# Two state-space chunks, or two input steps, in each interruption of TensorE's main stream

## The chip, the cores and the metric

The kernel runs on one core of one Trainium2 chip. The time is that of one launch on the device, in microseconds (us); lower is better. The core's engines are TensorE (PE), VectorE (DVE), ScalarE (ACT), GpSimd (POOL) and SyncE (SP). They run apart from each other and meet at semaphores. A chip run gives a median of several launches; a profile is one more launch, recorded instruction by instruction.

## The reference, cut to what matters

The program is a decoder trunk of two layers over 256 positions of width 2048. Layer 0 mixes positions with two kinds of attention, layer 1 with a state-space bank (S5) and a short convolution. After each mixer come a cross-attention into 256 memory tokens and a squared-ReLU MLP of width 8192. What the change touches is the state-space part:

```python
a_bar = jnp.exp(lam * step)
b_bar = ((a_bar - 1.0) / lam)[..., None] * lax.complex(b_re, b_im)
bu = jnp.einsum('blgc,gpc->blgp', uf, b_bar)
...
states = associative_scan(combine, (a_seq, bu))     # x[t] = a_bar * x[t-1] + bu[t]
y = jnp.einsum('blgp,gcp->blgc', states, c_mat).real + d_skip * uf
```

There are 64 groups of 16 channels and 64 complex states each. All else is matrix products of 256 rows with large weights.

## The kernel before

**Main stream.** Each weight matrix is read in slabs of 1 MB. A slab serves two *halves*; eight halves make a *unit*. For every half ACT copies the raw weights to a rounded part (`whi`, line 1282), DVE subtracts to get the remainder (`wlo`, line 1854), and TensorE multiplies with both (lines 635 to 637, or 1108 and 1111 in units that put the weights in the stationary place). The buffers hold four halves. So ACT may split half t only when TensorE is done with half t-4 (semaphore `half_used`), and TensorE may begin half t only when `wlo` of t is there (`lo_ready`). SP issues the slabs, each when `wlo` of the half that last used its place has been made.

**Side work.** A number t counts halves from a stage's start; after the split or the products of half t each engine calls what is due at t. Each engine's list is fixed in the program text, so an instruction that waits holds back all that stands behind it on its engine, the next split included.

**Tables.** The state-space tables depend only on parameters and are built beside the last chunks but one of layer 0's MLP (four chunks of four units, t = 0 to 127), in 16 *chunks* k of two group pairs each. For a chunk DVE makes the real parts in four pieces from t = 30 + 6k (`re_tables`, lines 1954 to 1973, semaphore `s5_re`) and POOL the imaginary parts (lines 2548 and 2779, `s5_im`). Both use the buffers k % 2. TensorE then visits (`s5_chunk`, after half 33 + 6k): 4 small fp32 matmuls into one bank of `at`, in 8 passes. At t = 37 + 6k ACT waits until the store of the chunk before has landed (`k_out`), copies half of the bank (line 1387), stores `et_d` and `ca_d` (lines 1389, 1392), waits until DVE has added the other half (lines 1932, 1935, `k_sum`), and stores `k_d` (two DMAs, line 1395). The buffers of chunk k are free for chunk k + 2 when TensorE has visited k and its stores have landed; SP loads the factors of chunk k (line 479) at t = 28 + 6k, once chunk k - 2 has used its own.

**Steps.** In layer 1's input projection (t from its first unit) TensorE makes the states' inputs in 8 *steps* (`s5_x`, after halves 27 to 34): 16 small matmuls, 32 passes, into one bank of `at`. ACT copies a step's bank three halves later in its own list (line 1353). SP loads the tables of step k (`et_d`, 0.5 MB, line 550) into a ring of three buffers, three steps ahead at most: step k waits for TensorE's step k - 3. The output steps (`s5_y`) already run two per visit, after halves 53, 55, and so on.

**Hidden sums.** In the MLP's second and third unit, DVE adds the two parts of the hidden products (line 2236), and ACT makes relu and two squares (lines 1639 to 1642), at fixed halves in the same lists (halves 2 and 4 of the unit).

Of the kernel before, what the change touches and what calls it, by code (L numbers as in the profile page):

```python
# [44 lines left out]
G, GC, ST = 64, 16, 64  # L45
Q = G // 2
T8 = 8
J = L // T8
# [57 lines left out]
def trunk(nc, x, mem, norm_mix, norm_xattn, norm_mlp, norm_mem, norm_final, ab_w_in, ab_b_forget,  # L106
# [4 lines left out]
    with ctx:  # L111
# [52 lines left out]
        etab = view(1024, 1024, "p (b q r w) -> p b q r w", b=2, q=2, r=2)  # L164
# [13 lines left out]
        cz = [view(at_, 576, "p (q r w) -> p q r w", q=2, r=2) for at_ in (7616, 10240)]  # L178
# [36 lines left out]
        S = view(2112, 2048, "p (r j q) -> p r j q", r=2, q=Q)  # L215
# [31 lines left out]
        at = ctx.enter_context(nc.psum_tensor("at", [P, 2, NB], F32))  # L247
# [4 lines left out]
        et_d = nc.dram_tensor("et_d", [P, Q, 2, GW], F32, kind="Internal").ap()  # L252
        ca_d = nc.dram_tensor("ca_d", [2, P, Q, GW], F32, kind="Internal").ap()
# [44 lines left out]
        s5_re, s5_im = sem("s5_re"), sem("s5_im")  # L298
# [33 lines left out]
        TAB_CHUNKS = (3, 4, 5, 6)  # L332
        FACTOR_T, STORE_T = (0, 2, 4), 16
        DVE_T = [32 + 6 * k - 2 for k in range(16)]
        CHUNK_T = [32 + 6 * k + 1 for k in range(16)]
        ROWS_T, SIN_T = 8, 29
        X8_T, SCAN_T, Y_T = 25, 39, 53
        SWAP_T = (49, 51, 52)
# [251 lines left out]
        def _(pe):  # L590
            p = Place()
# [186 lines left out]
            def s5_chunk(k):  # L778

                b = k % 2  # L780
                pe.wait_ge(s5_re, k + 1)
                pe.wait_ge(s5_im, k + 1)
                bank = open_at()
                for r in range(2):
                    for q in range(2):
                        ln = 2 * GC * (2 * r + q)
                        last = mm(bank[ln:ln + 2 * GC, 0:GW], eb[:, b, q, r, :], cz[b][:, q, r, 0:GW])
                close_at(last)
# [6 lines left out]
            def s5_tables(t):  # L795
                if t in FACTOR_T:
                    s5_factors(FACTOR_T.index(t))
                if t in CHUNK_T:
                    assert p.n["at"] == at_before_tab + CHUNK_T.index(t)
                    s5_chunk(CHUNK_T.index(t))  # L800

            for u in range(4):
                def after(i, u=u):
# [399 lines left out]
                close_at(last)  # L1203

            def s5_steps(t):
                if 0 <= t - X8_T - 2 < 8:
                    s5_x(t - X8_T - 2)
                if 0 <= t - Y_T < 16 and (t - Y_T) % 2 == 0:
                    s5_y(t - Y_T)
                    s5_y(t - Y_T + 1)  # L1210
# [49 lines left out]
        def _(act):  # L1260
# [87 lines left out]
            def at_copy(copies):  # L1348

                n = p.n["at"]  # L1350
                act.wait_ge(at_full, n + 1)
                for dst, src in copies(at[:, n % 2, :]):
                    last = act.activation(dst, src, ACT.Copy)
                last.then_inc(at_free[n % 2], 1)
                p.bump("at")
# [20 lines left out]
            def s5_tables(t):  # L1376

                if t - 4 in FACTOR_T:
                    at_copy(lambda bank: [(fput[FACTOR_T.index(t - 4)], bank)])
                if t - 4 not in CHUNK_T:  # L1380
                    return
                k = CHUNK_T.index(t - 4)
                b = k % 2
                n = p.n["at"]
                act.wait_ge(*((k_out, 32 * k) if k else (ksb_zero, 1)))
                act.wait_ge(at_full, n + 1)
                act.activation(ksb[:, 112:240], at[2 * 2 * GC:P, n % 2, 0:GW], ACT.Copy).then_inc(k_part, 1)
                p.bump("at")
                act.dma_start(et_d[:, 2 * k:2 * k + 2].rearrange("p q r w -> p (q r w)"),
                              etab[:, b].rearrange("p q r w -> p (q r w)")).then_inc(et_out[b], 16)  # L1390
                for r in range(2):
                    act.dma_start(ca_d[r, :, 2 * k:2 * k + 2], cz[b][:, :, r, GC:]).then_inc(ca_out[b], 16)
                act.wait_ge(k_sum, k + 1)
                for q in range(2):
                    act.dma_start(k_d.rearrange("c (s k q) w -> k q s c w", s=2, q=2)[k, q],
                                  ksb[2 * GC * q:2 * GC * (q + 1), :]).then_inc(k_out, 16)
# [308 lines left out]
            def s5_slots(t):  # L1705
                if t in SWAP_T:
                    swap_states(SWAP_T.index(t))
                k = t - 5 - X8_T
                if 0 <= k < 8:

                    at_copy(lambda bank: [
                        (S[:, r, :, 4 * k:4 * k + 4].rearrange("p j q -> p q j"),
                         bank[:, 0:8 * J].rearrange("p (q r j) -> p r q j", q=4, r=2)[:, r])
                        for r in range(2)])
                k = t - 3 - Y_T
                if 0 <= k < 16:
                    b = k % YB
                    if k >= YB:
                        act.wait_ge(y_out[b], 16 * (k // YB))
                    at_copy(lambda bank: [  # L1720
                        (Yc[:, b, :, q * GC:(q + 1) * GC], bank[2 * J * q:2 * J * (q + 1), 0:GW]
                         .rearrange("p (i c) -> p i c", i=T8)) for q in range(2)])
                    n = p.n["at"] - 1
                    act.wait_ge(at_free[n % 2], n // 2 + 1)
                    act.dma_start(y_d.rearrange("s (j i) n -> (s j) i n", i=T8)[
                        :, :, 2 * GC * k:2 * GC * (k + 1)], Yc[:, b]).then_inc(y_out[b], 16)
# [110 lines left out]
        def _(dve):  # L1837
# [87 lines left out]

            def re_tables(t):

                if t - 4 in CHUNK_T:
                    k = CHUNK_T.index(t - 4)
                    n = at_before_tab + k  # L1930
                    dve.wait_ge(k_part, k + 1)
                    dve.tensor_tensor(ksb[:, 112:240], at[0:2 * 2 * GC, n % 2, 0:GW], ksb[:, 112:240],
                                      ALU.add).then_inc(at_free[n % 2], 1)
                    dve.wait_ge(at_free[n % 2], n // 2 + 1)
                    dve.tensor_tensor(ksb[:, 112:112 + GC], ksb[:, 112:112 + GC], skip[:, k, :],
                                      ALU.add).then_inc(k_sum, 1)
                part = [(k, t - t0) for k, t0 in enumerate(DVE_T) if 0 <= t - t0 < 4]
                if not part:
                    return
                (k, part), = part  # L1940
                b, q0 = k % 2, 2 * k
                e, tv = etab[:, b, :, 0, :], vtmp3[:, 0:2 * P].rearrange("p (q w) -> p q w", q=2)
                t1 = vtmp2.rearrange("p (q i c) -> p q i c", q=2, i=9)
                t2 = vtmp.rearrange("p (q i c) -> p q i c", q=2, i=9)
                if part == 0:
                    if k == 0:
                        dve.wait_ge(prep_done, 1)
                        dve.wait_ge(tab_zero, 1)
                    if k >= 2:
                        dve.wait_ge(at_full, at_before_tab + k - 1)  # L1950
                        dve.wait_ge(et_out[b], 16 * (k // 2))
                    dve.wait_ge(f_in[b], 32 * (k // 2 + 1))
                    (br, bi), (pbr, pbi) = ((fac[:, b, f, :, r, :] for r in range(2)) for f in range(2))
                    dve.tensor_tensor(e, br, pbr, ALU.mult)
                    dve.tensor_tensor(tv, bi, pbi, ALU.mult)
                    (br, bi), (pbr, pbi) = last_parts(q0)
                    dve.tensor_tensor(vlast[:, 0], br, pbr, ALU.mult)
                    link(dve.tensor_tensor(vlast[:, 1], bi, pbi, ALU.mult))
                elif part == 1:
                    dve.tensor_tensor(e, e, tv, ALU.subtract)  # L1960
                    for s in range(2):
                        ln = slice(64 * s, 64 * s + 64)
                        last = dve.tensor_tensor(eb[ln, b, :, 0, s * GC:(s + 1) * GC], vlast[ln, 0], vlast[ln, 1],
                                                 ALU.subtract)
                    link(last)
                elif part == 2:
                    cr, ci, pr_, pi_ = table_parts(s5c, pw, q0, 9)
                    dve.tensor_tensor(t1, cr, pr_, ALU.mult)
                    link(dve.tensor_tensor(t2, ci, pi_, ALU.mult))
                else:  # L1970
                    if k >= 2:
                        dve.wait_ge(ca_out[b], 32 * (k // 2))
                    dve.tensor_tensor(cz[b][:, :, 0, :].rearrange("p q (i c) -> p q i c", i=9), t1, t2, ALU.add)\
                       .then_inc(s5_re, 1)
# [892 lines left out]
```

## Time and profile before

| | us |
|---|---|
| median of 3 runs | 2406.83 (2405.9 to 2407.12) |
| profiled execution | 2407.2 |
| its span, first to last instruction | 2405.4 |
| outside the span | 1.8 |
| busy in it: TensorE / VectorE / ScalarE / GpSimd | 2392.7 / 1490.1 / 1187.7 / 356.5 |

Times in the rows below count from the start of the span. Matmuls overlap: a row's length is longer than the time between two starts, so time on TensorE is read from start to start. A row ends in brackets with the idle time before it and what ended it, where there was some.

### The profile page before, as it was taken

How to read it: one execution, taken by the hardware profiler on the slowest of the kernel's cores; microseconds unless marked ns; L12 is line 12 of the kernel's file. 1: busy time of each engine (PE TensorE's matmuls, PEld its weight loads, DVE VectorE, ACT ScalarE, POOL GpSimd, SP SyncE). 2: the span in 40 equal slices, each digit the busy share in tenths (PEclk: the TensorE clock that was granted, in tenths of full speed). 3: DMA queues.
4: the chain of work that ended last, by engine and by line, in shares of the span. 5: the costliest groups of instructions: out<-in, count | busy, mean ns of one | idle time of the engine just before them, and what ended most of it. 6: DMA issues, size and time to landing. Idle time of an engine off the chain costs nothing.

```text
span 2405.4 us, 31978 instructions
## 1 busy us (share of the span) xinstructions
PE 2392.7 (99%) x12516; PEld 2021.8 (84%) x12516; DVE 1490.1 (62%) x1872; ACT 1187.7 (49%) x1580; POOL 356.5 (15%) x482
## 2 busy tenths in 40 slices
PE   9999999999999999999999999999999999999998
PEld 7878888889888888888888888888888888888887
DVE  5546554556665557888866657566755655555556
ACT  7544455546544444444445445556644444444444
POOL 0033120100564002554610100000000000000000
PEclk9999999999999999999999999999999999999999
DMA  8655565574566567787786768864665565566563
GB/s 311 215 171 188 182 203 174 163 205 144 191 193 191 190 195 225 238 259 234 252 276 191 224 211 258 266 201 149 202 193 191 188 191 189 187 190 192 191 192 123
DMA packets 338359, 488.56 MB, mean 203 GB/s; under 512 B 18948, under 2 KB 181668, under 8 KB 338116
## 3 DMA queue, kind: packets, MB, share of 16 engines
q1 hardware_dynamic: 312836, 460.42, 60.7%
q0 software_dynamic: 4256, 14.02, 2.1%
q10 hardware_dynamic: 21152, 12.53, 1.7%
q8 instruction: 78, 1.28, 0.2%
q14 instruction: 37, 0.30, 0.0%
HBM read 471.52 MB, written 19.60 MB: 204 GB/s over the span
## 4 chain that ended last, share of the span: by engine, by line
PE 96%; DVE 2%; ACT 1%; issue 0%; DMA 0%; ACTq 0%; SPq 0%; DVEq 0%
PE acc L635 20%; PE acc L637 19%; PE acc L636 19%; PE acc L1111 18%; PE acc L1108 9%; PE tp L702 2%; PE at L726 2%; PE acc L1076 1%; PE at L1076 1%; DVE wlo L1854 1%; PE tp L726 1%; PE acc L985 1%; PE acc L983 1%; PE acc L984 1%; ACT whi L1282 1%; PE at L1079 0%
## 5 line engine op out<-in xcount | busy, mean ns | idle before, releaser
L1854 DVE TENSOR_TENSOR wlo<-raw,whi 128x1024 fp32r<-128x1024 f32 x824 | 1047.9, 1275 | 795.1 <-ACT whi L1282 792.5
L1282 ACT ACTIVATE whi<-raw 128x1024 fp32r<-128x1024 f32 x824 | 870.1, 1060 | 975.7 <-PE acc L637 577.4
L635 PE MATMUL acc<-whi,yt_hi 128*128 128x512 f32 x1408 | 553.1, 393 | 0.2 <-DVE arena L2236 0.2
L637 PE MATMUL acc<-whi,yt_lo 128*128 128x512 f32 x1408 | 548.4, 390 | 0.0
L636 PE MATMUL acc<-wlo,yt_hi 128*128 128x512 f32 x1408 | 548.3, 389 | 0.0
L1111 PE MATMUL acc<-x,whi 128*128 128x512 f32 x1984 | 485.6, 392 | 0.0
L1111 PEld LDWEIGHTS acc<-x,whi 128*128 128x128 f32 x1984 | 361.4, 189 | 68.5 <-issue 0.8
L635 PEld LDWEIGHTS acc<-whi,yt_hi 128*128 128x128 f32 x1408 | 264.4, 188 | 56.4 <-issue 1.6
L637 PEld LDWEIGHTS acc<-whi,yt_lo 128*128 128x128 f32 x1408 | 264.3, 188 | 55.7
L636 PEld LDWEIGHTS acc<-wlo,yt_hi 128*128 128x128 f32 x1408 | 264.5, 188 | 53.1
L1108 PEld LDWEIGHTS acc<-x,wlo 128*128 128x128 f32 x1984 | 262.8, 191 | 15.3 <-issue 0.8
L1108 PE MATMUL acc<-x,wlo 128*128 128x256 f32 x1984 | 268.0, 283 | 0.0
L635 PE MATMUL acc<-whi,x 128*128 128x512 f32 x672 | 266.4, 396 | 0.0
L637 PE MATMUL acc<-whi,x 128*128 128x512 f32 x672 | 262.0, 390 | 0.0
L636 PE MATMUL acc<-wlo,x 128*128 128x512 f32 x672 | 261.8, 390 | 0.0
L2548 POOL TENSOR_TENSOR arena<-arena 128x32 f32<-128x32 f32 (+5 forms) x275 | 191.9, 698 | 321.5 <-DMA arena<-fp_d 181.4
L637 PEld LDWEIGHTS acc<-whi,x 128*128 128x128 f32 x672 | 126.1, 188 | 26.8
L635 PEld LDWEIGHTS acc<-whi,x 128*128 128x128 f32 x672 | 126.2, 188 | 26.6 <-issue 1.2
L636 PEld LDWEIGHTS acc<-wlo,x 128*128 128x128 f32 x672 | 126.3, 188 | 25.0
L2823 POOL TENSOR_TENSOR arena<-h,arena 128x1024 f32<-128x1024 f32 x2 | 5.7, 2850 | 660.4 <-DVE h L1891 660.4
L1891 DVE SCALAR_TENSOR_TENSOR h<-acc,rstd,h 128x512 f32<-128x512 f32 x124 | 87.1, 744 | 8.8 <-PE acc L637 8.7
L2236 DVE TENSOR_REDUCE arena<-acc 128x256 f32<-128x512 f32 x124 | 82.1, 681 | 0.0
(246 smaller groups left out, 1556.5 us busy)
## 6 DMA issues: line engine op xcount, KB each, us to landing
raw<-in_mlp_w SPq DMA_DIRECT2D x256, 1024.0 KB, 5.6
raw<-in_ab_w_in SPq DMA_DIRECT2D x56, 1024.0 KB, 5.0
raw<-in_cd_w_in SPq DMA_DIRECT2D x32, 1024.0 KB, 5.5
raw<-in_ab_w_out SPq DMA_DIRECT2D x16, 1024.0 KB, 5.2
raw<-in_cd_w_out SPq DMA_DIRECT2D x16, 1024.0 KB, 7.2
raw<-in_xa_wkv SPq DMA_DIRECT2D x15, 1024.0 KB, 9.8
raw<-in_xa_wq SPq DMA_DIRECT2D x16, 512.0 KB, 4.7
raw<-in_xa_wo SPq DMA_DIRECT2D x8, 512.0 KB, 4.6
```

Of the source, the lines that this page charges most:

```text
L635: pe.matmul(a, xh, whi[:, w, kk], start=opens and kk == 0, stop=False)
L636: pe.matmul(a, xh, wlo[:, w, kk], start=False, stop=False)
L637: last = pe.matmul(a, xl, whi[:, w, kk], start=False, stop=closes and kk == 1)
L702: last = pe.transpose(bank[:, kk * L + t * P:kk * L + (t + 1) * P], src[:, t, (2 * b + kk) * P:(2 * b + kk + 1) * P], ident[:, :])
L726: return pe.matmul(o, lhsT, rhs, start=start, stop=stop)
L1108: last = pe.matmul(o[:, 0:L], w_lo[:, kk, :], x2[:, 0, k0 + kk, :], start=False, stop=closes and kk == 7)
L1111: last = pe.matmul(o.rearrange("p (a n) -> p a n", a=2), w_hi[:, kk, :], x2[:, :, k0 + kk, :], start=i < 4 and kk == 0, stop=closes and kk ...
L1282: act.activation(split_weights(whi, kind, i), half_weights(raw, kind, i), ACT.Copy)\
L1854: dve.tensor_tensor(split_weights(wlo, kind, i), half_weights(raw, kind, i), split_weights(whi, kind, i).bitcast(F32), ALU.subtract).then_ ...
L1891: last = dve.scalar_tensor_tensor(out=hb, in0=acc[:, 2 * par_ + t, :], scalar=rstd[:, row, t:t + 1], in1=hb, op0=ALU.mult, op1=ALU.add)
L2236: ins = dve.tensor_reduce(hid[:, hh, :], bank.rearrange("p (a n) -> p n a", a=2), AX.X, ALU.add)
L2548: link(pool.tensor_tensor(o, a, b, op))
```

## The change

TensorE visits the chunks in pairs: chunks 2m and 2m + 1 after half 39 + 12m, where the odd one was visited before. ACT's and DVE's part at 37 + 6k splits in two. The stores of `et_d` and `ca_d` move to t = 36 + 6k and wait for the two writers (`s5_re`, `s5_im`) instead of for the visit. The copy, the sums and the store of `k_d` come at t = 43 + 12m for the even and 46 + 12m for the odd chunk, but never later than 126 and 127. TensorE's input steps run in pairs after halves 28, 30, 32 and 34, and ACT copies both banks in halves 31, 33, 35 and 37. No arithmetic, buffer or DMA is added or removed.

```diff
-        CHUNK_T = [32 + 6 * k + 1 for k in range(16)]
+        PAIR_T = [39 + 12 * m for m in range(8)]
+        KEEP_T = [36 + 6 * k for k in range(16)]
+        TAKE_T = [min(43 + 12 * (k // 2) + 3 * (k % 2), 126 + k % 2) for k in range(16)]
...
-                if t in CHUNK_T:
-                    assert p.n["at"] == at_before_tab + CHUNK_T.index(t)
-                    s5_chunk(CHUNK_T.index(t))
+                if t in PAIR_T:
+                    k = 2 * PAIR_T.index(t)
+                    assert p.n["at"] == at_before_tab + k
+                    s5_chunk(k)
+                    s5_chunk(k + 1)
...
-                if 0 <= t - X8_T - 2 < 8:
+                if 0 <= t - X8_T - 2 < 8 and (t - X8_T) % 2:
+                    s5_x(t - X8_T - 3)
                     s5_x(t - X8_T - 2)
...
-                if t - 4 not in CHUNK_T:
+                if t in KEEP_T:
+                    k = KEEP_T.index(t)
+                    b = k % 2
+                    act.wait_ge(s5_re, k + 1)
+                    act.wait_ge(s5_im, k + 1)
+                    act.dma_start(et_d[:, 2 * k:2 * k + 2].rearrange("p q r w -> p (q r w)"),
+                                  etab[:, b].rearrange("p q r w -> p (q r w)")).then_inc(et_out[b], 16)
+                    for r in range(2):
+                        act.dma_start(ca_d[r, :, 2 * k:2 * k + 2], cz[b][:, :, r, GC:]).then_inc(ca_out[b], 16)
+                if t not in TAKE_T:
                     return
-                k = CHUNK_T.index(t - 4)
-                b = k % 2
+                k = TAKE_T.index(t)
                 n = p.n["at"]
                 act.wait_ge(*((k_out, 32 * k) if k else (ksb_zero, 1)))
...
-                if 0 <= k < 8:
-
-                    at_copy(lambda bank: [
+                if 0 <= t - 5 - X8_T < 8 and (t - X8_T) % 2 == 0:
+                    for k in (t - 6 - X8_T, t - 5 - X8_T):
+                        at_copy(lambda bank, k=k: [
...
-                if t - 4 in CHUNK_T:
-                    k = CHUNK_T.index(t - 4)
+                if t in TAKE_T:
+                    k = TAKE_T.index(t)
```

**TensorE, the first input steps.** Before, one step (its first matmul and 15 more) stands between two halves, and the second step one half later:

```order
L637 MATMUL acc<-whi,x 128x512
L726 MATMUL at<-arena 64x32 [waits et_in0,u_in1,at_free1,u_in0,ut_zero]
L726 MATMUL at<-arena 64x32 x15
L635 MATMUL acc<-whi,x 128x512 [waits lo_ready]
L636 MATMUL acc<-wlo,x 128x512
```

Now (lines are numbered anew, 726 is 728 and 635 is 637):

```order
L639 MATMUL acc<-whi,x 128x512
L728 MATMUL at<-arena 64x32 [waits et_in0,u_in1,at_free1,u_in0,ut_zero]
L728 MATMUL at<-arena 64x32 x15
L728 MATMUL at<-arena,kvv 64x32 [waits at_free0,et_in1]
L728 MATMUL at<-arena,kvv 64x32 x15
L637 MATMUL acc<-whi,x 128x512 [waits lo_ready]
```

The second step follows the first directly; the chunks' visits change in the same way.

**ACT around half 82 of the tables** (`whi` is a split, the three 128x512 rows are relu and two squares). Before, from the split of half 79, with chunk 7's work behind it:

```order
L1282 ACTIVATE whi<-raw 128x1024 [waits half_used]
L1387 ACTIVATE arena<-at 64x128 [waits at_full,k_out]
L1389 DMA et_d<-arena 128x512
L1392 DMA ca_d<-arena 128x2x128 x2
L1395 DMA k_d<-arena 2x16x240 [waits k_sum]
L1395 DMA k_d<-arena 2x16x240
L1282 ACTIVATE whi<-raw 128x1024 [waits half_used,raw_landed0]
L1282 ACTIVATE whi<-raw 128x1024 [waits half_used]
L1282 ACTIVATE whi<-raw 128x1024 [waits half_used,raw_landed1]
L1639 ACTIVATE arena<-arena 128x512 [waits acc_free1]
L1641 ACTIVATE yt_hi<-arena 128x512 [waits hid_relu]
L1642 ACTIVATE arena<-arena 128x512
```

Now, from the store of chunk 6's `k_d` in half 79:

```order
L1404 DMA k_d<-arena 2x16x240
L1287 ACTIVATE whi<-raw 128x1024 [waits half_used,raw_landed0]
L1287 ACTIVATE whi<-raw 128x1024 [waits half_used]
L1287 ACTIVATE whi<-raw 128x1024 [waits half_used,raw_landed1]
L1400 ACTIVATE arena<-at 64x128 [waits at_full,k_out]
L1404 DMA k_d<-arena 2x16x240 [waits k_sum]
L1404 DMA k_d<-arena 2x16x240
L1648 ACTIVATE arena<-arena 128x512 [waits acc_free1]
L1650 ACTIVATE yt_hi<-arena 128x512 [waits hid_relu]
L1651 ACTIVATE arena<-arena 128x512
L1287 ACTIVATE whi<-raw 128x1024 [waits half_used]
```

The odd chunk's copy and store now stand in half 82, ahead of the squares and of the split of half 83.

**ACT at the end of the tables.** Before, splits and then chunk 15 in half 127:

```order
L1282 ACTIVATE whi<-raw 128x1024 [waits half_used]
L1282 ACTIVATE whi<-raw 128x1024 [waits half_used,raw_landed3]
L1282 ACTIVATE whi<-raw 128x1024 [waits half_used]
L1387 ACTIVATE arena<-at 64x128 [waits at_full,k_out]
L1389 DMA et_d<-arena 128x512
L1392 DMA ca_d<-arena 128x2x128 x2
L1395 DMA k_d<-arena 2x16x240 [waits k_sum]
L1395 DMA k_d<-arena 2x16x240
L1282 ACTIVATE whi<-raw 128x1024 [waits half_used,raw_landed0]
```

Now, from the split of half 126:

```order
L1287 ACTIVATE whi<-raw 128x1024 [waits half_used,raw_landed3]
L1390 DMA et_d<-arena 128x512 [waits s5_im,s5_re]
L1393 DMA ca_d<-arena 128x2x128 x2
L1400 ACTIVATE arena<-at 64x128 [waits at_full,k_out]
L1404 DMA k_d<-arena 2x16x240 [waits k_sum]
L1404 DMA k_d<-arena 2x16x240
L1287 ACTIVATE whi<-raw 128x1024 [waits half_used]
L1400 ACTIVATE arena<-at 64x128 [waits at_full,k_out]
L1404 DMA k_d<-arena 2x16x240 [waits k_sum]
L1404 DMA k_d<-arena 2x16x240
L1287 ACTIVATE whi<-raw 128x1024 [waits half_used,raw_landed0]
```

Chunk 14 is taken in half 126 and chunk 15 in half 127, with one split between them; the second waits on `k_out` for the first one's stores.

## Rows read from the trace of the kernel before

**Rows 1.** The page: span, and busy time of the engines (share, instructions).
```profile
span 2405.4 us, 31978 instructions
...
PE 2392.7 (99%) x12516; PEld 2021.8 (84%) x12516; DVE 1490.1 (62%) x1872; ACT 1187.7 (49%) x1580; POOL 356.5 (15%) x482
```

**Rows 2.** Timeline of TensorE, halves 122 to 124 (start, length, line, tiles):
```profile
1211.84 0.39 PE L637 MATMUL acc<-whi,yt_lo 128*128 128x512 f32 x1
...
1214.56 0.39 PE L637 MATMUL acc<-whi,yt_lo 128*128 128x512 f32 x1
1214.88 0.43 PE L726 MATMUL at<-arena 128*32 128x128 f32 x8
...
1217.88 0.39 PE L637 MATMUL acc<-whi,yt_lo 128*128 128x512 f32 x1
```

**Rows 3.** Timeline of TensorE, halves 33 to 35 of the tables:
```profile
956.53 1.11 PE L1108 MATMUL acc<-x,wlo 128*128 128x256 f32 x8
...
959.86 1.12 PE L1108 MATMUL acc<-x,wlo 128*128 128x256 f32 x8
...
962.65 2.08 PE L1108 MATMUL acc<-x,wlo 128*128 128x256 f32 x16
```

**Rows 4.** Timeline of TensorE, two input steps; then by line (ns min/median/max):
```profile
1395.32 1.12 PE L726 MATMUL at<-arena 128*64 128x32 f32 x32
...
1399.32 1.12 PE L726 MATMUL at<-arena,kvv 128*64 128x32 f32 x32
...
L726 PE MATMUL at<-arena,kvv x96: 222/223/243, 1399.3 to 1425.1; 128*64 128x32 f32 x96
```

**Rows 5.** Timeline of TensorE, inside an output visit of two steps:
```profile
1506.23 0.41 PE L726 MATMUL at<-arena 128*32 128x128 f32 x8
1506.45 0.41 PE L726 MATMUL at<-yt_hi,arena 128*32 128x128 f32 x8
```

**Rows 6.** Timeline of ACT and its queue, halves 127 and 128:
```profile
1215.95 0.26 ACT L1387 ACTIVATE arena<-at 64x128 f32<-64x128 f32 x1
...
1217.73 1.20 ACTq L1395 DMA_DIRECT2D k_d<-arena  x2
1219.03 1.06 ACT L1282 ACTIVATE whi<-raw 128x1024 fp32r<-128x1024 f32 x1 [2.82 <-PE acc L637]
```

**Rows 7.** Timeline of DVE, the two sums of chunk 15:
```profile
1217.22 0.28 DVE L1932 TENSOR_TENSOR arena<-at,arena 64x128 f32<-64x128 f32 x1
1217.53 0.17 DVE L1935 TENSOR_TENSOR arena<-arena 64x16 f32<-64x16 f32 x1
```

**Rows 8.** Timeline of POOL, which waits for the last store of `k_d`:
```profile
1225.42 6.15 POOL L2787 DMA_DIRECT2D t_d<-k_d  x8 [26.08 <-DMA k_d<-arena]
```

**Rows 9.** By tile: landing of the 24 DMAs that write or read `et_d`:
```profile
DMA to landing us min/median/max: 3.4/6.0/8.6
```

**Rows 10.** Timeline of ACT, half 82 of the tables:
```profile
1089.81 0.63 ACT L1639 ACTIVATE arena<-arena 128x512 f32<-128x512 f32 x1 [1.79 <-DVE arena L2236]
...
1091.54 1.04 ACT L1282 ACTIVATE whi<-raw 128x1024 fp32r<-128x1024 f32 x1
```

**Rows 11.** Timeline of DVE, halves 80 to 83 of the tables:
```profile
1086.13 0.45 DVE L1968 TENSOR_TENSOR arena<-arena 128x288 f32<-128x288 f32 x1
1086.49 1.00 DVE L1969 TENSOR_TENSOR arena<-arena 128x288 f32<-128x288 f32 x1
...
1092.25 1.27 DVE L2236 TENSOR_REDUCE arena<-acc 128x256 f32<-128x512 f32 x2
1093.45 1.29 DVE L1854 TENSOR_TENSOR wlo<-raw,whi 128x1024 fp32r<-128x1024 f32 x1
```

**Rows 12.** Timeline of TensorE: start of half 80, end of half 81:
```profile
1089.83 0.50 PE L635 MATMUL acc<-whi,yt_hi 128*128 128x512 f32 x1 [0.21 <-DVE arena L2236]
...
1095.22 0.39 PE L637 MATMUL acc<-whi,yt_lo 128*128 128x512 f32 x1
```

**Rows 13.** Timeline of POOL, chunk 14 but for its last operation:
```profile
1171.41 10.09 POOL L2548 TENSOR_TENSOR arena<-arena 128x256 f32<-128x256 f32 x9 [5.04 <-DMA ca_d<-arena]
```

More of the change, by code:

```diff
@@ L1388, in s5_tables @@
                 p.bump("at")
[L1389 to L1392, printed above, removed]
                 act.wait_ge(k_sum, k + 1)
@@ L1707, in s5_slots @@
                     swap_states(SWAP_T.index(t))
-                k = t - 5 - X8_T
-                if 0 <= k < 8:
-                    at_copy(lambda bank: [
-                        (S[:, r, :, 4 * k:4 * k + 4].rearrange("p j q -> p q j"),
-                         bank[:, 0:8 * J].rearrange("p (q r j) -> p r q j", q=4, r=2)[:, r])
-                        for r in range(2)])
+                if 0 <= t - 5 - X8_T < 8 and (t - X8_T) % 2 == 0:
+                    for k in (t - 6 - X8_T, t - 5 - X8_T):
+                        at_copy(lambda bank, k=k: [
+                            (S[:, r, :, 4 * k:4 * k + 4].rearrange("p j q -> p q j"),
+                             bank[:, 0:8 * J].rearrange("p (q r j) -> p r q j", q=4, r=2)[:, r])
+                            for r in range(2)])
                 k = t - 3 - Y_T
```

## The prediction

> **What bounds the kernel now.** I read the page first, then TensorE's timeline around each kind of visit, then ACT's, DVE's and POOL's at the places to which the change moves work. The page shows TensorE busy for 2392.7 of 2405.4 us [rows 1]: whatever leaves TensorE's list leaves the time, as long as ACT and DVE keep delivering splits. Others matter only where they come too late. That happens in few places now; one is a wait of 0.21 us for a DVE sum at the start of half 80 of the tables [rows 12].
>
> **What a visit costs.** A half of the main stream takes 2.72 us from end to end, and 3.32 with a chunk's visit in it: 0.60 [rows 2]. In units with stationary weights it is 3.33 against 2.79: 0.54 [rows 3]. The visit's own passes are the smaller part: eight in 0.43 us, the last one's length included, and they begin 0.32 us after the last main matmul, where main ones follow at 0.23 [rows 2]. The rest is the change from one form of matmul to the other and back. An input step costs 4.00 - 2.72 = 1.28 [rows 2, 4], its passes from first to last start 1.12 - 0.22 = 0.90 [rows 4].
>
> **What a second one in the same visit costs.** The output visits show it, since they hold two steps: their groups of eight small passes, as many as a chunk has and of its form, follow each other at 0.22 us [rows 5]. So a second chunk costs 0.22. A second input step costs its passes alone, 0.90 and one more interval, 0.93; the bounds are 0.90 and 1.12 [rows 4].
>
> **Removed and added on TensorE.** Eight chunk visits go (after halves 33, 45, 57 and so on to 117), four in each kind of unit: 4 x 0.60 + 4 x 0.54 = 4.56. Eight second chunks come: 8 x 0.22 = 1.76. Four step visits go, 4 x 1.28 = 5.12, and four second steps come, 4 x 0.93 = 3.72. The gain is 2.80 + 1.40 = 4.20 us, between 3.4 and 4.3 with the bounds.
>
> **What the moved work costs, and where it is hidden.** ACT is three halves ahead of TensorE at best, so work in its list at half t has about 7 us (four halves, less the split before it and the split and subtraction after it) before TensorE stands still. In most chunks the moved parts fit: the three stores go out one half earlier, beside a split, and POOL, which may begin an even chunk only after the paired visit, needs 10.1 us and a last operation [rows 13] where five halves (14 us) pass until ACT asks for the result. SP waits for the same chunk before it loads factors four chunks on; that is at about the time at which it loads them now. The odd chunk's copy waits for the landing of the even one's `k_d`, three halves after its issue; 8 us cover the 6.0 of a median store [rows 9]. Two places do not fit.
>
> *The end of the tables.* Let E be the end marker of half 123, 1214.56 [rows 2]. Chunk 14's bank is full at E + 0.75 (0.32 and 0.43). Copy (0.26) and sums (0.51, starts 1217.22 to 1217.73) with the hand-overs bring the store to E + 1.6 [rows 6, 7]; the second of its two DMAs starts 0.6 later, at E + 2.2. The split of half 127 comes between. Chunk 15's copy then waits for this landing. Its bounds: 3.4 us, the fastest DMA of the rows, and 8.6, the slowest [rows 9]. Nearest is the same store of chunk 15: its second DMA started at about 1218.3 and POOL went on at 1225.42, 7.1 us later, POOL's own start included [rows 6, 8]. I take 6.3, between that and the median of 6.0. So E + 8.5; copy and sums make E + 9.4, the two issues 1.3 (1217.73 to 1219.03), the split 1.06 and the subtraction 1.29 [rows 6, 11] make E + 13.0. TensorE wants half 128 at E + 3.32 + 0.22 + 3 x 2.72 + 0.1 = E + 11.8. It waits 1.2 us; 0 at the low bound, 3.5 at the high one.
>
> *Half 82.* Chunk 7's copy, sums and store now stand ahead of the relu and squares there. DVE reaches its sums for the chunk only behind the hidden sums, which end at 1093.45 [rows 11]. Plus 0.51 for the sums, 1.3 for the issues, 1.73 for relu and squares (1089.81 to 1091.54 [rows 10]), 1.04 for the split and 1.29 for the subtraction: 1099.3. TensorE's visit after half 81 is gone, so it ends half 82 at 1095.22 + 2.72 = 1097.9 and wants the next 0.2 later [rows 12]: 1.2 us of waiting, 0 to 2.2 by how far behind DVE is. (The visits before it shift all engines alike.)
>
> *Elsewhere.* Halves 58 and 106 have the same arrangement with half a microsecond to spare, and POOL now works two chunks in a row. I add 0.4 us, between 0 and 2.
>
> **The sum.** -4.2 + 1.2 + 1.2 + 0.4 = -1.4 us against the profiled 2407.2, so 2405.8. The median of the runs lies 0.4 below the profiled execution: 2405.4. A measurement of this kernel can tell about 0.2% (4.8 us) from no change, so faster means below 2402.0 and slower above 2411.6. Even the full gain of 4.2 stays inside.
>
> **Two rules weighed.** The last store took up to 7.1 us to land [rows 8]. The Trainium skill (DMA: Bandwidth & Descriptors, section Anatomy of one DMA) gives a fixed cost of some 2.0 us and the bytes; by that, 2.1 us for these 30 KB, the wait at the end would vanish and the sum would be -2.6. The trace disagrees, with 3.4 as its shortest landing [rows 9].
>
> DVE's products of 128x288 take 0.45 and 1.00 us one after the other, in a stretch in which POOL computes a chunk too [rows 11]. The Trainium skill (SBUF — State Buffer, section SBUF: two separate sides) says that VectorE and GpSimd lock a shared pair of ports for a whole instruction. It speaks against this change, which lets POOL run about 22 us without a break.
>
> **The rivals.**
>
> *Full gain.* The store lands sooner and DVE comes to half 82 less late, since POOL is idle in the halves before each paired visit. For it: splits now catch up where ACT's stores are spread over two halves. Against it: both waits are chains of measured rows. All 4.2 us stay: 2402.6.
>
> *Slower by DVE behind POOL.* POOL's two chunks in a row cover the starts of units at halves 40, 56, 64, 80, 88 and 104. Each product that meets POOL costs 0.55 more [rows 11], two to four of them stand in the way of a sum that frees a bank: 1.1 us at each of four starts is 4.4, on top of the 2.4 of the two waits: -4.2 + 2.4 + 4.4 = +2.6, 2409.4. It turns to a loss once the waits exceed 4.2 in all. Against it: today's POOL already overlaps half of these starts, and one shows 0.21.
>
> *The second step waits for its table.* The loads of steps 3, 5 and 7 may begin only when steps 0, 2 and 4 are over, 1.4 us after the half's end, and are wanted 0.32 + 0.93 after the end of the half two on, that is 2 x 2.72 + 1.28 + 0.93 + 1.25 = 8.9: 7.5 us for a load. The median is 6.0, the slowest 8.6 [rows 9]. At the slowest it is 1.1 each, 3.3 in all, and the sum is +1.9: 2408.7. Against it: the change then does what it says only in the tables; but the landings of 8.6 belong to moments with several loads at once.
>
> **How the numbers follow.** The forecast, 2405.4 with a range of its own of 2403.5 to 2407: 0.5. Full gain: 0.2. Slower behind POOL: 0.2. Late tables: 0.1. The range from 2402.4 to 2408.8 holds the full gain and most of the last two, and leaves out some 2 in 10. Beyond 0.2% on the fast side lies only a full gain in which today's waits vanish too (0.04); on the slow side, waits of over 9 us (0.05); the rest is no difference, 0.91.
>
> **What would show it.** Eight visits of 16 small passes and four of 64, with 0.22 and 0.93 us for the second part, show the first term. ACT's copy in half 127 with an idle time that ends at a landing of `k_d`, and a gap in TensorE's stream at half 128, show the second; a gap at half 83 with DVE's `wlo` behind a late `whi` the third. No gap at either means the full gain. Gaps at unit starts that end at a DVE sum mean the POOL rival; a gap inside an input visit means late tables. The prediction is wrong if these gaps add up to less than 1 or more than 5 us.

## The result: 11 us slower

| | before | after |
|---|---|---|
| median of 6 runs, us | 2406.45 (2405.9 to 2407.12) | 2417.52 (2416.66 to 2418.51) |
| profiled execution, us | 2407.2 | 2418.18 |
| its span, us | 2405.4 | 2416.4 |

The ratio is 1.0046, with a 95% interval of 1.0035 to 1.0056: slower by 0.46%, outside the range of the prediction and on the side to which it gave 0.05.

The page of the changed kernel answers to [rows 1]. TensorE's busy time is what it was (2392.7), in a span that is 11.0 us longer. So nothing was added to TensorE's work; it stands still for longer.

```profile
span 2416.4 us, 31994 instructions
...
PE 2392.6 (99%) x12516; PEld 2023.0 (84%) x12516; DVE 1490.5 (62%) x1872; ACT 1188.8 (49%) x1580; POOL 333.8 (14%) x482
```

The waits of TensorE in the tables (930 to 1245 us; total, count and longest, in us) name DVE each time. Of before, the same view holds the one wait of [rows 12].

```profile
engine line waited for: us in total, times, longest us
PE acc L637 <- DVE h L1899: 3.8, 2, 2.2
PE acc L637 <- DVE arena L2244: 2.8, 2, 1.4
PE acc L1115 <- DVE h L1899: 1.4, 2, 0.8
PE acc L1115 <- DVE arena L2244: 1.4, 1, 1.4
PE acc L637 <- DVE wlo L1862: 1.0, 1, 1.0
PE acc L1115 <- DVE wlo L1862: 0.8, 1, 0.8
```

L1899 is the addition to `h` at a unit's start, L2244 the hidden sums, L1862 the subtraction `wlo`. These are 11.2 us. A wait also leaves TensorE slower behind it, which the view doesn't count. So I compared halves: from the start of a half's last main matmul to that of the next half's, for halves 30 to 135, less the same time in a kernel without gaps (e3 below), corrected by what the visits cost. A remainder of more than 0.12 us is called a gap here, and stands under the number of the half that came late.

| kernel | gaps, us (half: size) | sum |
|---|---|---|
| before | 56: 0.33, 80: 0.51 | 0.8 |
| after | 47: 0.45, 48: 1.69, 56: 3.87, 57: 0.28, 72: 0.31, 80: 1.65, 83: 1.31, 96: 0.97, 104: 1.62, 107: 1.07, 119: 0.32, 120: 1.86, 128: 1.07 | 16.5 |

TensorE's own saving came as forecast. A removed chunk visit gave 0.53 to 0.60 us, a second chunk cost 0.21 to 0.23, and the input steps gave 1.39 in all, without a wait. The rows answer to [rows 2, 4]: the half with a visit of two chunks takes 1229.15 - 1225.61 = 3.54, where one with a single chunk took 3.32; and a second step begins 0.96 after the first.

```profile
1225.61 0.39 PE L639 MATMUL acc<-whi,yt_lo 128*128 128x512 f32 x1
1225.93 0.65 PE L728 MATMUL at<-arena 128*32 128x128 f32 x16
...
1229.15 0.39 PE L639 MATMUL acc<-whi,yt_lo 128*128 128x512 f32 x1
...
1410.37 1.12 PE L728 MATMUL at<-arena 128*64 128x32 f32 x32
1411.33 1.10 PE L728 MATMUL at<-arena,kvv 128*64 128x32 f32 x32
```

The account closes to 0.4 us: -4.24 saved, -0.84 for the two old gaps (which the 16.46 contain), +16.46, that is +11.4; the spans differ by 11.0.

### Where TensorE stands still

**Half 56, 3.87 us.** TensorE's timeline in the changed kernel (start, length, line, tiles):

```profile
1021.32 0.39 PE L639 MATMUL acc<-whi,yt_lo 128*128 128x512 f32 x1
1023.93 0.50 PE L637 MATMUL acc<-whi,yt_hi 128*128 128x512 f32 x1 [2.22 <-DVE h L1899]
...
1025.35 0.63 PE L639 MATMUL acc<-whi,yt_lo 128*128 128x512 f32 x1
1025.78 0.63 PE L637 MATMUL acc<-whi,yt_hi 128*128 128x512 f32 x1
```

DVE's timeline just before:

```profile
1017.19 1.85 DVE L1862 TENSOR_TENSOR wlo<-raw,whi 128x1024 fp32r<-128x1024 f32 x1 [1.36 <-ACT whi L1287]
1018.97 0.99 DVE L1976 TENSOR_TENSOR arena<-arena 128x288 f32<-128x288 f32 x1
1019.88 0.99 DVE L1977 TENSOR_TENSOR arena<-arena 128x288 f32<-128x288 f32 x1
1020.90 1.65 DVE L1862 TENSOR_TENSOR wlo<-raw,whi 128x1024 fp32r<-128x1024 f32 x1
1022.48 1.40 DVE L1899 SCALAR_TENSOR_TENSOR h<-acc,rstd,h 128x512 f32<-128x512 f32 x2
```

And POOL's:

```profile
1010.54 6.51 POOL L2556 TENSOR_TENSOR arena<-arena 128x256 f32<-128x256 f32 x9 [18.96 <-PE at L728]
...
1018.14 8.18 POOL L2556 TENSOR_TENSOR arena<-arena 128x256 f32<-128x256 f32 x9 [0.18 <-POOL arena L2787]
```

In the kernel before, the same DVE operations, with POOL idle from 1010.0 to 1018.39, read:

```profile
1016.10 1.23 DVE L1854 TENSOR_TENSOR wlo<-raw,whi 128x1024 fp32r<-128x1024 f32 x1 [1.85 <-ACT whi L1282]
1017.24 0.45 DVE L1968 TENSOR_TENSOR arena<-arena 128x288 f32<-128x288 f32 x1
1017.61 0.45 DVE L1969 TENSOR_TENSOR arena<-arena 128x288 f32<-128x288 f32 x1
1018.10 1.22 DVE L1854 TENSOR_TENSOR wlo<-raw,whi 128x1024 fp32r<-128x1024 f32 x1
1019.24 1.40 DVE L1891 SCALAR_TENSOR_TENSOR h<-acc,rstd,h 128x512 f32<-128x512 f32 x2
```

From the first `wlo` to the addition it was 3.14 us, and is 5.29. The four operations ahead of the addition are longer by 0.62, 0.54, 0.54 and 0.43, 2.13 in all. ACT was no later than before: the first `wlo` begins 4.13 us ahead of the last matmul of half 55 (1021.32), where it began 4.18 ahead of it (1020.28), behind one hand-over that held ACT for 4.75 us here and for 4.49 before. And the kernel before had no slack at this place (its gap was 0.33), so all of the 2.13 reaches TensorE; the view shows 2.22 in brackets.

The rest of the 3.87 is the clock: 0.33 + 2.13 + 1.4 = 3.86. The stretches of 1 us (busy share and count of PE, PEld, DVE, ACT, POOL; then the granted clock, the DMA share, GB/s) show it at 1.00 before, and at 0.50, the lower level of 1.2 GHz, in three stretches (1025 to 1028) that begin 1.1 us after the pause of 2.6 us. Matmuls there start 0.43 us apart (1025.35 and 1025.78 above) instead of 0.23: seven intervals, 1.4 us.

```profile
1022.00:1023.00 1.00, 0.00 (x0) 0.00 (x0) 1.00 (x2) 0.00 (x0) 0.89 (x2) 1.00 0.00 0
...
1024.00:1025.00 1.00, 1.00 (x5) 0.82 (x6) 1.00 (x2) 0.00 (x0) 0.92 (x2) 1.00 0.81 183
1025.00:1026.00 1.00, 1.00 (x4) 0.81 (x3) 1.00 (x2) 0.00 (x0) 0.99 (x1) 0.50 0.92 270
...
1027.00:1028.00 1.00, 1.00 (x4) 0.76 (x3) 0.57 (x3) 0.00 (x0) 0.21 (x1) 0.50 1.00 305
```

**Halves 47 and 48.** Here ACT is the one that comes late; its lead, by which its splits run ahead of TensorE, is used up. Its timeline shows chunk 1's copy (due at half 46), its store and the next split; `ACTq` is ACT's DMA queue:

```profile
986.15 0.26 ACT L1400 ACTIVATE arena<-at 64x128 f32<-64x128 f32 x1
990.74 1.19 ACTq L1404 DMA_DIRECT2D k_d<-arena  x2
991.98 1.06 ACT L1287 ACTIVATE whi<-raw 128x1024 fp32r<-128x1024 f32 x1 [5.57 <-PE acc L1112]
```

DVE makes the two sums at 990.16 and 990.47, behind a `wlo` of 1.72 us and two products of 0.96 and 0.99, all beside POOL. ACT waits for the sums before it can issue the store, and no split leaves for 5.6 us. The name in brackets is the wait that came last by the profile; the copy and the store between show what held ACT. Such a hand-over, copy to DVE to store, stood in every sixth half before, and held ACT for 3.4 to 5.1 us each time but the last. Now there are two of them within three halves, and then none for nine.

**Half 83, 1.31 us, and its twin 107.** ACT's timeline again, with the copy of chunk 7 first:

```profile
1093.51 0.28 ACT L1400 ACTIVATE arena<-at 64x128 f32<-64x128 f32 x1 [1.04 <-DMA k_d<-arena]
1099.56 1.20 ACTq L1404 DMA_DIRECT2D k_d<-arena  x2
1100.80 0.63 ACT L1648 ACTIVATE arena<-arena 128x512 f32<-128x512 f32 x1 [7.02 <-issue]
...
1102.52 1.99 ACT L1287 ACTIVATE whi<-raw 128x1024 fp32r<-128x1024 f32 x2
```

TensorE's:

```profile
1104.88 0.50 PE L637 MATMUL acc<-whi,yt_hi 128*128 128x512 f32 x1 [0.97 <-DVE wlo L1862]
```

This is the chain that the prediction worked out, in the order that it gave, for 7.0 us between the copy and the relu.

**Half 128, 1.07 us.** ACT's timeline at the end of the tables:

```profile
1226.48 0.28 ACT L1400 ACTIVATE arena<-at 64x128 f32<-64x128 f32 x1 [2.04 <-PE at L728]
1227.31 1.20 ACTq L1404 DMA_DIRECT2D k_d<-arena  x2
...
1231.51 0.28 ACT L1400 ACTIVATE arena<-at 64x128 f32<-64x128 f32 x1 [1.89 <-DMA k_d<-arena]
1232.34 1.19 ACTq L1404 DMA_DIRECT2D k_d<-arena  x2
1233.63 2.96 ACT L1287 ACTIVATE whi<-raw 128x1024 fp32r<-128x1024 f32 x3 [1.84 <-issue]
```

And TensorE's:

```profile
1238.46 2.12 PE L1115 MATMUL acc<-x,whi 128*128 128x512 f32 x8 [0.76 <-DVE h L1899]
```

Chunk 15's copy does wait for the landing of chunk 14's `k_d`. But that landed 3.6 us after its second DMA started (about 1227.9), and TensorE waits for an addition to `h`, which stands on DVE behind two subtractions.

### The profile page after: what moved, and what is told of

It is laid out like the page before. It is cut to its first block, busy times and chain, and to the rows that moved or that the text cites. A ratio compares the mean times of both kernels' runs of the same rounds, so it can differ in the third digit from the quotient of the medians.

```text
span 2416.4 us, 31994 instructions
## 1 busy us (share of the span) xinstructions
PE 2392.6 (99%) x12516; PEld 2023.0 (84%) x12516; DVE 1490.5 (62%) x1872; ACT 1188.8 (49%) x1580; POOL 333.8 (14%) x482
## 4 chain that ended last, share of the span: by engine, by line
PE 90%; DVE 6%; ACT 2%; issue 1%; ACTq 1%; DMA 0%; SPq 0%; DVEq 0%
PE acc L637 18%; PE acc L639 18%; PE acc L638 18%; PE acc L1115 17%; PE acc L1112 9%; DVE wlo L1862 3%; PE tp L704 2%; PE at L728 1%; ACT whi L1287 1%; PE acc L1080 1%; PE at L1080 1%; ACTq L1404 1%; PE tp L728 1%; PE acc L989 0%; PE acc L987 0%
## 5 line engine op out<-in xcount | busy, mean ns | idle before, releaser
L1862 DVE TENSOR_TENSOR wlo<-raw,whi 128x1024 fp32r<-128x1024 f32 x824 | 1042.5, 1269 | 801.4 <-ACT whi L1287 798.5
L2556 POOL TENSOR_TENSOR arena<-arena 128x32 f32<-128x32 f32 (+5 forms) x275 | 172.4, 627 | 352.4 <-DMA arena<-fp_d 180.4
L1899 DVE SCALAR_TENSOR_TENSOR h<-acc,rstd,h 128x512 f32<-128x512 f32 x124 | 87.2, 745 | 8.8 <-PE acc L639 8.8
L2244 DVE TENSOR_REDUCE arena<-acc 128x256 f32<-128x512 f32 x124 | 82.2, 683 | 0.0
```

Source lines behind the costliest of these rows:

```text
L1862: dve.tensor_tensor(split_weights(wlo, kind, i), half_weights(raw, kind, i), split_weights(whi, kind, i).bitcast(F32), ALU.subtract).then_ ...
L1899: last = dve.scalar_tensor_tensor(out=hb, in0=acc[:, 2 * par_ + t, :], scalar=rstd[:, row, t:t + 1], in1=hb, op0=ALU.mult, op1=ALU.add)
L2244: ins = dve.tensor_reduce(hid[:, hh, :], bank.rearrange("p (a n) -> p n a", a=2), AX.X, ALU.add)
L2556: link(pool.tensor_tensor(o, a, b, op))
```

## Experiments

Two causes are in question. One is POOL, whose chunks now run in pairs beside DVE's work at the starts of units (theory A in the expectations; A1 and A2 are two forms of it). The other lies in ACT's list: at first that the odd copy comes too soon after the even one (theory B), and from e9 on the hand-over itself, in which ACT stands until DVE has made the sums (theory H). Late weights are no candidate: in the tables of the changed kernel the view of waits has none of ACT's for the landing of a slab. Gaps are those of the table above, taken in one profile of each kernel. Medians and ratios are against the kernel before on the same chip.

### The steps alone (e1)

```diff
+                if 0 <= t - X8_T - 2 < 8 and (t - X8_T) % 2:
+                    s5_x(t - X8_T - 3)
                     s5_x(t - X8_T - 2)
```

This and the two copies in one half, in the kernel before.

> The kernel before with the input steps in pairs and nothing else. Both theories of the loss (A: GpSimd's two chunks in a row slow VectorE; B: the odd chunk's copy comes too soon after the even one's) place it in the tables, so this part alone should give its own term: four visits of 1.28 us go and four second steps of 0.93 come, -1.4 us, 2405.0 against 2406.4, with no new gap on TensorE between halves 27 and 40 of the projection. If the steps take part in the loss the time is above 2406.4.

Measured: 2405.09 (11 runs) against 2406.79 (17 runs); 0.9995, interval 0.9985 to 1.0004. In the steps' part of the profile 1.39 us are gone, and no wait came. The two gaps of before (0.8) were absent in this profile, though nothing was changed there: that much varies. The loss is in the tables alone.

### POOL's work left out (e2 and e3)

In the kernel after (e2) and, as a control, in the kernel before (e3):

```diff
+                if k >= 2:
+                    pool.memset(gtmp[:, 0:1], 0.0).then_inc(s5_im, 1)
+                    pool.wait_ge(s5_im, k + 1)
+                    continue
```

> The changed kernel in which GpSimd makes the imaginary tables of chunks 0 and 1 only; for the 14 others it keeps its waits and signals but leaves the 11 operations out (so these tables are not the reference's). Theory A (VectorE behind GpSimd): the gaps at halves 48, 56, 80, 96, 104 and 120 (10.8 us against the kernel before) go; those at 83 and 128 stay, the sum falls by 8 to 10 us to some 2408. Theory B (the copies too close together): all gaps stay within a third, the time stays above 2413.

> The kernel before with the same operations of GpSimd left out: the control for the run before it. It shows what sharing costs when GpSimd's chunks are spread. Theory A: little, because the two waits of today (0.3 and 0.5 us at halves 56 and 80) are all there is: -0.8 us, 2405.6. Theory B says the same. A fall of several us would mean that GpSimd delays more than the gaps show.

Measured, one run each: 2403.03 for e2, 2405.89 for e3. In e2 a gap of 1.05 at half 128 is all that is left of 16.5; e3 has none. The DVE operations of half 56 in e2:

```profile
1013.70 1.23 DVE L1862 TENSOR_TENSOR wlo<-raw,whi 128x1024 fp32r<-128x1024 f32 x1 [1.86 <-ACT whi L1287]
1014.84 0.45 DVE L1976 TENSOR_TENSOR arena<-arena 128x288 f32<-128x288 f32 x1
1015.21 0.45 DVE L1977 TENSOR_TENSOR arena<-arena 128x288 f32<-128x288 f32 x1
1015.70 1.23 DVE L1862 TENSOR_TENSOR wlo<-raw,whi 128x1024 fp32r<-128x1024 f32 x1
```

So POOL's operations are needed for 15.4 of the 16.5 us, the gap at half 83 among them. That is more than either theory had said (2408, or above 2413). The one at 128 isn't POOL's. Without POOL the change gives what TensorE's list promises: 4.2 less 1.05 is 3.2, and e2 is 2.9 below e3.

### The odd copy three halves later (e4)

```diff
-        TAKE_T = [min(43 + 12 * (k // 2) + 3 * (k % 2), 126 + k % 2) for k in range(16)]
+        TAKE_T = [min(43 + 12 * (k // 2) + 6 * (k % 2), 126 + k % 2) for k in range(16)]
```

> The changed kernel with the odd chunk's copy, sums and store six halves after the even one's (49, 61, 73 and so on) instead of three; the last two stay at 126 and 127. GpSimd still works two chunks in a row. Theory A: the gaps at the starts of units with an addition or sum (56, 80, 104) stay within a quarter; only the gap at 83 and part of that at 48 go: about -3 us, 2414. Theory B: the gaps at 48, 83, 96, 107 and 120 go, 7 us, and the time is 2409 to 2411.

Measured: 2414.4 (6 runs), 1.0034 (1.0022 to 1.0046). The time is theory A's, but the gaps fit neither. Those at 47, 48, 83, 107 and 119 are gone; 56 (2.55), 80 (1.61), 96 (0.39), 104 (0.83) and 120 (0.37) stay, all but 80 clearly smaller; 128 has grown to 4.44, with the clock low behind it. Sum 10.5. Two hand-overs close together are part of the cause, not all of it.

### POOL's odd chunk later (e5)

```diff
+                if k >= 3 and k % 2:
+                    pool.wait_ge(lo_ready, 288 + 47 + 12 * ((k - 3) // 2) + 1)
```

> The changed kernel with one wait added on GpSimd: it begins the odd chunk 2m + 3 only when VectorE has made the remainder of half 47 + 12m, so that its two chunks are some eight halves apart, as they were before, and not in a row. Nothing is removed: the same operations share the same port pair. Theory A1 (it is the row of two that hurts: VectorE has no half in between to catch up): the gaps at 48, 56, 80, 96, 104 and 120 shrink from 11 us to 0 to 2 and the time is 2405 to 2408. Theory A2 (any overlap with the starts of units hurts, wherever it lies): the time stays above 2411, with gaps at other unit starts.

Measured: 2416.27 (5 runs), 1.0039 (1.0026 to 1.0052). The gaps of 56, 80 and 104 shrink to 0.99, 0.69 and 0.65, but 48 (1.59) stays, 96 has grown to 1.49 and 120 to 5.03, and others open: 85 and 110, where POOL now works, and 117. Sum 14.5. That POOL works two chunks *in a row* is not what costs; theory A1, which said so, fell. The gaps fit with POOL at work beside DVE wherever ACT's lead is short.

### The last pair taken apart (e6), and both (e7)

```diff
-        PAIR_T = [39 + 12 * m for m in range(8)]
+        PAIR_T = [39 + 12 * m for m in range(7)] + [117, 123]
-        TAKE_T = [min(43 + 12 * (k // 2) + 3 * (k % 2), 126 + k % 2) for k in range(16)]
+        TAKE_T = [43 + 12 * (k // 2) + 3 * (k % 2) for k in range(14)] + [121, 127]
```

> The changed kernel with the last pair undone: chunk 14 is visited after half 117 and taken at 121, chunk 15 after 123 and taken at 127. The gap at half 128 (1.07 us) goes, since chunk 15 no longer waits for stores issued one half before; one visit more costs 0.39. GpSimd's row of two stays, so the gaps at unit starts stay: 2416.5 to 2417.

> Both edits together: GpSimd's chunks spread and the last pair undone. If theory A1 holds this is the version that should beat both kernels: -4.2 + 0.4 for the visit that comes back, and up to 1 us of waits at unit starts: 2402.5 to 2404. If A2 holds it stays above 2410.

Measured: 2417.2 for e6 (one run), in which the gap at 128 is gone and the others stay (14.7). 2414.85 for e7, which is e5 and e6 together (6 runs), 1.0035 (1.0022 to 1.0047), with 11.2 of gaps; the 2402.5 to 2404 of theory A1 fell here too. The end of the tables is worth about one us; spreading POOL's work is no cure with it either.

### The early stores alone (e8)

The block with `KEEP_T` in the kernel before, and nothing else:

```diff
+        KEEP_T = [36 + 6 * k for k in range(16)]
...
-                act.dma_start(et_d[:, 2 * k:2 * k + 2].rearrange("p q r w -> p (q r w)"),
-                              etab[:, b].rearrange("p q r w -> p (q r w)")).then_inc(et_out[b], 16)
```

> The kernel before with the stores of et_d and ca_d at 36 + 6k behind their two writers, and nothing else of the change. It tells whether that part costs by itself. TensorE's list is untouched, GpSimd's chunks stay six halves apart, begun about one half sooner: within 0.5 us of before, 2406 to 2407.

Measured: 2408.24 (one run), 1.2 above the upper end of what I expected, with gaps of 1.45 at 56, 0.27 at 80 and 0.51 at 104. Stores that land sooner let POOL start sooner (1014.83 instead of 1018.39), and that lays it over the start of half 56. A single run is no more than a hint, but the gaps are those of the changed kernel, in small.

### The store of `k_d` one half behind the copy (e9)

```diff
+        PUT_T = [t + 1 for t in TAKE_T[:15]]
...
+                if t in PUT_T:
+                    put_k(PUT_T.index(t))
...
-                act.wait_ge(k_sum, k + 1)
```

`put_k` holds the wait for the sums and the two DMAs, unchanged. Chunk 15 keeps them with its copy. So one split leaves between the copy and the wait for DVE, and POOL still works two chunks in a row.

> The changed kernel with the store of k_d one half behind the copy in ScalarE's list (the last one stays with its copy), so that ScalarE does not stand between its copy and its store until VectorE has reached its two sums. Theory H (the hand-over: ScalarE gives away some 4 us of its lead at each copy, twice in three halves now, and VectorE, slowed by GpSimd, cannot make it good before the next unit starts): the gaps at 47, 48, 56, 80, 83, 96, 104, 107 and 120 fall from 15 us to under 4; the one at 128 stays or grows to 2: 2405 to 2407. Theory A alone (VectorE behind GpSimd, whatever ScalarE does): the gaps at 56, 80 and 104, 7 us, stay: above 2411.

Measured: 2404.3 (10 runs), 0.999 (0.9981 to 0.9999), 13 us below the changed kernel. ACT at the place of halves 47 and 48:

```profile
985.09 0.25 ACT L1409 ACTIVATE arena<-at 64x128 f32<-64x128 f32 x1
985.82 1.06 ACT L1288 ACTIVATE whi<-raw 128x1024 fp32r<-128x1024 f32 x1 [0.48 <-PE acc L1113]
989.23 1.19 ACTq L1385 DMA_DIRECT2D k_d<-arena  x2
```

The split leaves 0.7 us after the copy starts, instead of 5.8. Gaps: 80 (0.15), 104 (0.15), 120 (0.89) and 128 (1.42), 2.6 in all. POOL is busy over the start of half 56 as it was (52.3 to 58.4, counted in halves), and half 56 has no gap:

```profile
1008.35 7.48 POOL L2563 TENSOR_TENSOR arena<-arena 128x256 f32<-128x256 f32 x9 [14.83 <-PE at L729]
...
1016.89 8.00 POOL L2563 TENSOR_TENSOR arena<-arena 128x256 f32<-128x256 f32 x9
```

Thus the hand-over is needed for 13.9 of the 16.5 us, and POOL for 15.4. They are not parts of a sum: without the hand-over ahead of the split POOL's work leaves 2.6 us of gaps, and without POOL's work the hand-overs leave 1.05. The landing of the even chunk's `k_d`, for which the odd copies wait, is not what costs: seven copies wait for it in e9, 11.1 us in all by the view of waits, and six in the changed kernel, 9.6. The two issues (1.2 us) moved together with the wait; no run separates them.

### A version that beats both (e10), and the same idea without chunk pairs (e11)

e10 is e9 with the copies six halves apart (chunk 13's four) and the last two chunks visited apart (`put_k` as there):

```diff
-        PAIR_T = [39 + 12 * m for m in range(8)]
+        PAIR_T = [39 + 12 * m for m in range(7)] + [117, 123]
-        TAKE_T = [min(43 + 12 * (k // 2) + 3 * (k % 2), 126 + k % 2) for k in range(16)]
+        TAKE_T = [43 + 12 * (k // 2) + 6 * (k % 2) for k in range(13)] + [119, 123, 127]
+        PUT_T = [t + 1 for t in TAKE_T[:15]]
```

e11 is the kernel before with the steps of e1 and the store of `k_d` in the half behind its copy.

> As the run before it, and the odd chunk's copy six halves after the even one's; the last two chunks are visited alone after 117 and 123 and copied at 123 and 127 (chunk 13 at 119). Theory H: no gap above 0.5 us is left and the time is -4.2 + 0.4 for one more visit, with the two waits of the kernel before gone as well: 2402 to 2403.5, faster than both. Theory A alone: above 2409.

> The kernel before with the input steps in pairs (its tables unpaired, GpSimd as before) and the store of k_d one half behind the copy. Theory H: the two waits of before at halves 56 and 80 go for good: -1.4 - 0.8, 2404.2. Theory A alone: 2405, as the steps in pairs gave.

Measured: e10 2402.58 (11 runs), 0.9982 (0.9973 to 0.9991), gaps of 0.3 in all; e11 2404.67 (11 runs), 0.999 (0.9981 to 0.9999), no gaps. No run of one reaches into the runs of the other (2402.16 to 2402.96, and 2404.31 to 2404.87). So the pairs of chunks are worth 2.1 us once nothing waits for them. By unit costs it is 2.5 for seven pairs, less 0.3 of gaps. POOL in e10, with two chunks in a row over the same unit start and a span of 2400.5 us:

```profile
1008.28 7.48 POOL L2564 TENSOR_TENSOR arena<-arena 128x256 f32<-128x256 f32 x9 [14.87 <-PE at L729]
1015.84 0.91 POOL L2795 TENSOR_TENSOR arena<-arena 128x288 f32<-128x288 f32 x1
1016.83 9.03 POOL L2564 TENSOR_TENSOR arena<-arena 128x256 f32<-128x256 f32 x9
```

## Why the prediction was wrong

**What bounds, and TensorE's terms.** Right. The terms of -2.80 and -1.40 measured -2.85 and -1.39.

**The second step's table.** The rival of late tables fell: no wait inside an input visit, in after or in e1.

**Half 82 and 83.** Forecast 1.2, measured 1.31. The sums came at 1099.05, behind the hidden sums, as the chain said. But e2 shows that this wait too needs POOL. The chain held that only in so far as its start, 1093.45, was read where POOL was at work too. And its twin, half 107 with 1.07, was put down under "elsewhere" with half a microsecond to spare.

**The end of the tables.** Forecast 1.2, measured 1.07, and this is no proof of the chain. The landing was 3.6 us, near the low bound, by which the chain gave no wait. Left out was the addition to `h` for which TensorE waits there. Two errors cancelled, and the number was luck.

**Elsewhere: the step that failed.** "In most chunks the moved parts fit", and 0.4 us, between 0 and 2. It measured 14.1 (16.5 less 1.3 and 1.1), or 13.2 above what was there before. The prediction's own sign of being wrong, gaps of more than 5 us, came true with 16.5. Four things in this step were wrong.

- The budget of 7 us was held against each copy alone. With DVE's queue ahead of the sums, one hand-over holds ACT for 3.6 to 7.0 us (5.57 and 7.02 in the rows above; only the last two, behind POOL's work, take 1.8). Two of them three halves apart draw on the same lead. e9 shows that the hand-overs are needed: the wait moved behind one split, and 13.9 us go. e4 shows what their closeness is worth: the gaps at 47, 48, 83, 107 and 119 (4.8 us) go when the hand-overs stand six halves apart, and others shrink. The gap at 56 needs no second hand-over; it is the one of before with POOL laid over it.
- It counted the hand-over as "copy 0.26 and sums 0.51 with the hand-overs". The time until DVE *reaches* the sums was priced at half 82 only. It is there at every chunk.
- DVE's longer operations beside POOL were kept for a rival, not put in the sum.
- "8 us cover the 6.0 of a median store" did not hold: the even chunk's store left late, and five odd copies ahead of the last pair stood until it had landed (1.04 us in the row of half 83). By e9 this was not what cost.

**The rival behind POOL** had the sign, and the right places in part (56, 80, 104), but gave +2.6 against the +11 measured. It priced two stretched products, 1.1 us, at each start. At half 56 four operations stretch by 2.13, the two subtractions among them. It didn't price the clock (1.4 us there), nor the splits that come late through ACT. Its evidence against itself, that one start with such an overlap shows only 0.21, was read the wrong way: a start where DVE is just in time is a start without slack, not one that bears more.

**The full gain** needed ACT to win back its lead where its stores are spread. e10 and e2 come near it (2402.58 and 2403.03), each by taking away one of the two causes.

**The rules weighed.** The Trainium skill (SBUF — State Buffer, section SBUF: two separate sides) says that VectorE and GpSimd lock a shared pair of ports, and I gave that too little weight. The rows agree with it in direction: 0.45 against 0.99 us for a product, 1.23 against 1.85 for a subtraction, and both short in e2, with POOL's work gone. That the ports are the cause, and not something else that the two share, no run here separates. On the landing, the traces stay above the 2.0 us that the Trainium skill gives (DMA: Bandwidth & Descriptors, section Anatomy of one DMA), with 2.8 to 6.5 us from the start of the second DMA of a `k_d` in the changed kernel. That figure of the page is for DMAs that GpSimd issues, and these are issued by ScalarE, so the comparison is a loose one.

## What to carry to other kernels

When a change moves a step whose engine waits for another engine in the middle, price the time until the other engine *reaches* its part, out of its queue at that place and with its operations at their slowest, and then add up all such steps inside one lead; a lead is spent once. Let work that others wait for leave before the wait: one split between the copy and the store turned +11 us into -2.6. And a place where TensorE is already late by a little, 0.33 us at half 56, has nothing to spare: the 2.13 us that the change laid over it were paid in full.

## What the runs showed of the hardware

- One pause of 2.6 us between two matmuls, behind a long stretch of full work, was followed, from 1.1 us on, by three us at a granted clock of 0.50, and cost 1.4 us more than the pause itself. Behind the wait of 1.36 us at half 80 the clock stayed at 1.00.
- DVE beside POOL: at half 56 a subtraction of 128x1024 took 1.65 and 1.85 us instead of 1.23, and a product of 128x288 0.99 instead of 0.45. An addition that reads a bank of TensorE's took 1.40 for two in either case. In e9 and e10 the same two products took 0.50 and 0.51 beside POOL, so the overlap does not always cost.
- The landings of `k_d` in the changed kernel took 2.8 to 6.5 us, from the start of the second of the same two DMAs.
